# Queries and keys of the second block: where the squares, the gains and the norm's factor are applied

## The reference

```python
q, k, v, p = jnp.split(h @ w_in, [...], axis=-1)
q = rope_2d(rms_norm_2(q.reshape(bsz, seq, N_Q_HEADS, HEAD_DIM), q_gain), row_ang, col_ang)
k = rope_2d(rms_norm_2(k.reshape(bsz, seq, N_KV_HEADS, HEAD_DIM), k_gain), row_ang, col_ang)
...
kc = rms_norm_2(kc.reshape(bsz, n_ctx, N_KV_HEADS, HEAD_DIM), k_gain)     # context keys: no rotation
# rms_norm_2(x, gain) = x * rsqrt(mean(x*x) + EPS) * gain, per head
# rope_1d: x1, x2 = halves; concat(x1*cos - x2*sin, x2*cos + x1*sin)
```

## Time and profile before

| | |
|---|---|
| median of 3 runs | 2244.4 us (2242.2 to 2245.37) |
| the profiled execution | 2244.1 us, its span 2242.5 us |
| PE busy | 2044.5 us (91%) |
| DVE, ACT, POOL busy | 794.9, 580.6, 715.6 us |
| mean granted TensorE clock | 0.951 of full speed |

### The profile page before, as it was taken

How to read it: one execution, slowest core, us unless ns; L and a number is a source line. 1 busy time by engine, 2 the same in 40 slices (tenths; PEclk the granted TensorE clock), 3 DMA queues, 4 the chain that set the end, 5 groups by cost and what they waited for, 6 DMA issues and landing times. The chain is left out here.

```text
span 2242.5 us, 23210 instructions
## 1 busy us (share of the span) xinstructions
PE 2044.5 (91%) x7824; PEld 1099.2 (49%) x7824; DVE 794.9 (35%) x1596; ACT 580.6 (26%) x1205; POOL 715.6 (32%) x1055
## 2 busy tenths in 40 slices
PE   7999999999999999999997697995999699778995
PEld 5555555555564555555542355653444344344442
DVE  1434534432123444433315358533222300442223
ACT  3234331234113442221511114521111211111110
POOL 4766766756766676600000031000110100001101
PEclk9999999999999999999998798996999799878997
DMA  7234343234343244360112600016995621055994
GB/s 301 84 113 150 133 145 119 95 127 145 127 150 111 90 166 144 119 266 38 48 75 104 220 16 22 1 46 279 349 366 210 226 75 38 0 226 227 369 366 165
DMA packets 71119, 339.29 MB, mean 151 GB/s; under 512 B 8760, under 2 KB 10230, under 8 KB 56694
## 3 DMA queue, kind: packets, MB, share of 16 engines
q1 hardware_dynamic: 38502, 217.48, 25.7%
q0 software_dynamic: 27920, 103.82, 13.1%
q10 hardware_dynamic: 4608, 16.78, 1.8%
HBM read 292.97 MB, written 45.09 MB: 151 GB/s over the span
## 5 line engine op out<-in xcount | busy, mean ns | idle before, releaser
L386 PE MATMUL psA<-gB,ring 128*128 128x512 f32 x1024 | 455.1, 597 | 0.0
L324 POOL TENSOR_TENSOR wm<-wm,cs 128x256 f32<-128x256 f32 x448 | 266.3, 627 | 135.4 <-DMA wm<-in_mod_w 134.8
L386 PEld LDWEIGHTS psA<-gB,ring 128*128 128x128 f32 x1024 | 189.5, 190 | 223.8 <-issue 223.8
L328 POOL TENSOR_TENSOR wm<-wm 128x256 f32<-128x256 f32 x336 | 243.8, 753 | 31.1 <-issue 23.1
L378 PE MATMUL psA<-ring,gB 128*128 128x384 f32 (+1 forms) x768 | 242.9, 474 | 1.2 <-ACT gB L665 1.2
L378 PEld LDWEIGHTS psA<-ring,gB 128*128 128x128 f32 x768 | 144.6, 190 | 92.0 <-issue 6.8
L1326 POOL DMA_INDIRECT arena<-xs_scratch,idx x4 | 3.9, 965 | 446.7 <-issue 446.7
L842 DVE COPY probT<-psT 128x512 f32<-128x512 f32 x96 | 65.9, 686 | 159.4 <-PE psT L367 159.4
L1460 PE MATMUL psSO<-wreg,arena 128*128 128x512 f32 x256 | 115.3, 593 | 1.9 <-DVE arena L1986 1.9
L1445 PE MATMUL psA<-wreg,arena 128*128 128x512 f32 x256 | 114.9, 602 | 0.0
L1402 PE MATMUL psA<-wreg,mixT 128*128 128x512 f32 x256 | 113.1, 602 | 1.6 <-issue 0.8
(11 more groups left out here) (283 smaller groups left out, 2790.6 us busy)
## 6 DMA issues: line engine op xcount, KB each, us to landing
wm<-in_mod_w POOLq DMA_DIRECT2D x56, 1024.0 KB, 7.9
wreg<-in_w_gu SPq DMA_DIRECT2D x16, 2048.0 KB, 8.6
wreg<-in_w_dn SPq DMA_DIRECT2D x32, 1024.0 KB, 12.3
ring<-in_w_qk SPq DMA_DIRECT2D x24, 1024.0 KB, 4.9
mixT<-in_w_gu SPq DMA_DIRECT2D x8, 2048.0 KB, 8.6
aT<-in_w_gu SPq DMA_DIRECT2D x8, 2048.0 KB, 8.5
ys_scratch<-arena ACTq DMA_DIRECT2D x32, 512.0 KB, 9.9
ring<-in_w_v SPq DMA_DIRECT2D x8, 1536.0 KB, 6.9
```

Source lines behind the costliest of these rows:

```text
L324: nc.gpsimd.tensor_tensor(wm[:, b, k], wm[:, b, k], c_all[:, k].to_broadcast([P, MCH]), ALU.mult)
L328: nc.gpsimd.tensor_tensor(wm[:, b, k], wm[:, b, k], wm[:, b, n + k], ALU.add)
L386: m = nc.tensor.matmul(psA[:, n % 2, :], w(i), src[:, k, :], start=(i == 0), stop=(i == len(ks) - 1))
```

## The change

Four things are done in another way.

1. ACT squares the values straight from the projection's bank, in front of the copy out of the same bank: eight heads for a query tile, two for a key tile, each into one of the two buffers of `sq` in turn. The squares behind the last copy are gone.
2. DVE multiplies the gains into the rotation's tables, once, before the first reduction: in place for the queries (`rope2`), into a second table in `xm` for the keys (`rope_k`). The sine tables take the gains of the swapped half.
3. DVE reduces and rotates each tile as soon as ACT has copied it, with temporaries in `xm` (`by_cos`, `by_sin`) in place of `sq`. Context keys get the gain only.
4. The factor of the norm is applied last, to tiles that are already rotated; a rotation is linear, and the factor is one number per head and token.

```diff
+    by_cos, by_sin = flat_xm[:, 0:512], flat_xm[:, 640:1152]
+    rope_k = flat_xm[:, 1280:1792].rearrange("p (c t n) -> p c t n", c=2, t=NT)
...
+            def squares(n, src, cols, i):
+                act.wait_ge(a_ready, n + 1)
+                if i >= 2:
+                    act.wait_ge(sq_used, i - 1)
+                nc.scalar.activation(sq[:, i % 2, cols], src, ACT.Square).then_inc(sq_ready, 1)
+
+            for t in range(NT):
+                squares(t, psA[:, t % 2, :], slice(0, 512), t)
                 copy_out(t, qk[:, t, 0:512], psA[:, t % 2, :])
             for n in range(NT + CT):
                 bank = psA[:, n % 2, :]
-                act.wait_ge(a_ready, A_KV + n + 1)
+                squares(A_KV + n, bank[:, 0:P], slice(512, 640), NT + n)
...
-            act.drain()
-            for t in range(NT):
-                if t >= 2:
-                    act.wait_ge(sq_used, t - 1)
-                nc.scalar.activation(sq[:, t % 2, :], qk[:, t, :], ACT.Square).then_inc(sq_ready, 1)
-            act.wait_ge(sq_used, 3)
-            nc.scalar.activation(sq[:, 0, 0:CT * P], kc[:, :, :].rearrange("p t n -> p (t n)"), ACT.Square).then_inc(sq_ready, 1)
-            act.wait_ge(sq_used, 5)
+            act.wait_ge(sq_used, 2 * NT + CT)
             nc.scalar.activation(rmsh[:], ssh[:], ACT.Sqrt, scale=1.0 / HD, bias=eps[:]).then_inc(hd_rms, 1)
...
+            dve.wait_ge(tab_loaded, 16 * 8)
+            dve.wait_ge(t_ready, T_CTX)
+            for i, table in ((1, rope_k), (0, rope2)):
+                for t in range(NT):
+                    nc.vector.tensor_tensor(table[:, 0, t, :], rope2[:, 0, t, :], gains[:, i, :], ALU.mult)
+                    for c in range(2):
+                        nc.vector.tensor_tensor(swapped_halves(table[:, 1, t, :])[:, :, c, :], swapped_halves(rope2[:, 1, t, :])[:, :, c, :],
+                                                swapped_halves(gains[:, i, :])[:, :, 1 - c, :], ALU.mult)
+                dve.drain()
...
+            def roped(x, n, table, t):
+                a, b = by_cos[:, 0:n * HD], by_sin[:, 0:n * HD]
+                nc.vector.tensor_tensor(heads(a, n), heads(x, n), across(table[:, 0, t, :], n), ALU.mult)
...
+            for t in range(NT):
+                sum_squares(t, slice(0, 512), 8, 10 * t)
+                dve.wait_ge(a_copied, t + 1)
+                roped(qk[:, t, 0:512], 8, rope2, t)
+            for t in range(NT):
+                sum_squares(NT + t, slice(512, 640), 2, 10 * t + 8)
+                dve.wait_ge(a_copied, A_KV + t + 1)
+                roped(qk[:, t, 512:640], 2, rope_k, t)
+            for t in range(CT):
+                sum_squares(2 * NT + t, slice(512, 640), 2, 40 + 2 * t)
+            dve.wait_ge(a_copied, A_CTX + CT)
+            nc.vector.tensor_tensor(all_kc, all_kc, across(gains[:, 1, :], 4), ALU.mult)
             dve.wait_ge(hd_rms, 1)
             nc.vector.reciprocal(rsh[:], rmsh[:])
             dve.drain()
+            nc.vector.tensor_tensor(all_kc, all_kc, down(rsh[:, 40:44], 4), ALU.mult)
             for t in range(NT):
                 nc.vector.tensor_tensor(heads(qk[:, t, :], 10), heads(qk[:, t, :], 10), down(rsh[:, 10 * t:10 * t + 10], 10), ALU.mult)
             dve.drain()
...
             dve.sem_inc(qk_ready, 1)
```

More of the change, by code:

```diff
@@ L2033, in heads @@
                 return x.rearrange("p (h n) -> p h n", h=n)
[L2035 to L2044, removed]
             def across(x, n):
@@ L2050, in down, with swapped_halves @@
                 return x.rearrange("p (h o) -> p h o", o=1).to_broadcast([P, n, HD])
+            def swapped_halves(x):
+                return x.rearrange("p (b c n) -> p b c n", b=2, c=2)
+            dve.wait_ge(tab_loaded, 16 * 8)
[7 more added lines that the diff above has]
+                dve.drain()
@@ new lines, in sum_squares @@
+            def sum_squares(i, cols, n, at):
+                dve.wait_ge(sq_ready, i + 1)
+                nc.vector.tensor_reduce(ssh[:, at:at + n], heads(sq[:, i % 2, cols], n), AX.X, ALU.add).then_inc(sq_used, 1)
+            def roped(x, n, table, t):
+                a, b = by_cos[:, 0:n * HD], by_sin[:, 0:n * HD]
+                nc.vector.tensor_tensor(heads(a, n), heads(x, n), across(table[:, 0, t, :], n), ALU.mult)
+                halves = "p (h b c n) -> p h b c n"
+                sizes = dict(h=n, b=2, c=2)
+                for c in range(2):
+                    sin = table[:, 1, t, :].rearrange("p (o b c n) -> p o b c n", o=1, b=2, c=2)[:, :, :, c, :]
+                    nc.vector.tensor_tensor(b.rearrange(halves, **sizes)[:, :, :, c, :], x.rearrange(halves, **sizes)[:, :, :, 1 - c, :],
+                                            sin.to_broadcast([P, n, 2, 16]), ALU.mult)
+                dve.drain()
+                nc.vector.tensor_tensor(x, a, b, ALU.add)
+                dve.drain()
@@ L2052, in _ @@
+            dve.wait_ge(a_copied, A_CTX + CT)
+            all_kc = heads(kc[:, :, :].rearrange("p t n -> p (t n)"), 4)
+            nc.vector.tensor_tensor(all_kc, all_kc, across(gains[:, 1, :], 4), ALU.mult)
+            dve.wait_ge(hd_rms, 1)
+            nc.vector.reciprocal(rsh[:], rmsh[:])
+            dve.drain()
+            nc.vector.tensor_tensor(all_kc, all_kc, down(rsh[:, 40:44], 4), ALU.mult)
             for t in range(NT):
                 nc.vector.tensor_tensor(heads(qk[:, t, :], 10), heads(qk[:, t, :], 10), down(rsh[:, 10 * t:10 * t + 10], 10), ALU.mult)
-            nc.vector.tensor_tensor(all_kc, all_kc, down(rsh[:, 40:44], 4), ALU.mult)
@@ L2055, in _ @@
             dve.drain()
[L2056 to L2073, removed]
```

## The result

The changed kernel takes 2232.64 us (median of 6 runs, 2230.63 to 2235.8), the kernel before, run beside it, 2245.56 (6 runs). The ratio is 0.9943, 95% interval 0.9927 to 0.9959: 0.6% faster, 12.9 us by the medians. 2231.3 had been forecast, in a range of 2228.5 to 2235.5. The profiled execution took 2230.95, its span 2229.4 (mean granted clock 0.955), against 2242.5 before: 13.1 us less.

What follows compares the result with a forecast made beforehand. PE, busy 91%, was taken to bound the kernel with its gaps; 11.8 us for the qk_ready wait plus 1.2 for the clock made 13.0 saved, so 2231.3 us, range 2228.5 to 2235.5.

Steps and rivals of the forecast that it cites:

- The wait for `qk_ready`: PE's wait for DVE before the transposes of keys and queries: it goes whole, 11.8 us saved.
- Squares: ACT's squares ahead of its copies cost the copy's price, 0.60 us for 512 columns, 0.28 for 128; PE not held.
- Tables: DVE's 24 added products on the rotation tables take 5 us, at most 9.8, and cost PE 0.
- A query tile: DVE's reduction and rotation per query tile take 3.3 to 5.5 of 6.9 us, under PE's projections.
- A key tile: DVE's five instructions per key tile take 2.4 of 3.5 us, under PE's projections.
- The clock: PE's transposes up to scores(0) run at the full clock: 1.2 us saved, ends 0 and 1.9.
- The chain of copies: DVE's copies after the first transpose: second key copy at 1.8 us, queries 1 at 4.0, scores(0) at 4.5.
- Early attention runs cold: Rival, chance 0.14: the clock falls in attention's thin start, costing at most 2.9 us; time 2232.5 to 2235.4.
- Two of the signs named in advance: Granted clock 1.00 through transposes and attention; the same length from scores(0) to the end.
- Not passed on: Rival, chance 0.04: a later stage waits for something not shifted, so the gain is lost; 2238 to 2244.
- slower: Rival, chance 0.03: DVE crowded during projections, ACT's squares hold the banks, PE stalls 23.6 us; 2255.
- POOL beside attention: POOL's last four adds run beside attention's start and may hold a DVE division: 0, at most 1 us.

Runs made afterwards that it cites:

- e4: Kernel before, with 13 unread products of 128x512 put into PE's wait for qk_ready; 2246.09 us, ratio 1.0004.
- e5: Changed kernel, with 2 and 3 unread products of 128x512 in PE's two idle stretches around scores(1); 2231.37 us, ratio 0.9935.
- e10: Changed kernel timed again, nothing altered, beside the kernel before on another chip; 2232.66 us, ratio 0.9949.
- e9: Changed kernel, with 38 unread adds of 512 columns on POOL while DVE does its per-tile work; 2235.85 us, ratio 0.9965.
- e2: Kernel before, with one added line: POOL waits for qk_ready before its pooling sums; 2232.26 us, ratio 0.9941.
- e7: Changed kernel, with PE's transposes, scores(0) and scores(1) placed between the pooling products; 2225.44 us, ratio 0.9910.

## Why the prediction was right

**The wait for `qk_ready`, 11.8 us.** Right: 11.96 in the profile. Its parts held. Squares cost 0.60 and 0.28, the copy's price. Tables took 3.0 us (1266.33 to 1269.3), under the 5 taken and far from the bound of 9.8. A query tile took 2.7 us, below the 3.3 to 5.5: the reduction, the product and the add of 512 columns took 0.69 each, where the prediction had 0.79 and 0.82 from rows of 640, and two sine products of 256 took 0.75, where its lower end had 0.82. A key tile took 1.3 of the 2.4. `qk_ready` came at 1319.9, forecast 1319.5, in a run whose pooling products ended 0.9 later.

**The clock, 1.2 us.** Right where it was looked for: 1.45 in the changed kernel, 1.4 alone in e4. The chain of copies that the prediction wrote out is what the DVE rows show, a little faster: both key copies done 1.7 us behind the first transpose (forecast 1.8), queries 1 at 3.6 (4.0), `scores(0)` at 4.25 (4.5).

**Early attention runs cold.** This was a rival with 0.14 and 0 to 2.9 us, taken as an alternative to the forecast. It came about together with it: 1.32 us, shown by e5 to be the clock. The failed step is "against it: it stayed at 0.99 through this very stretch". Before, that stretch came right behind a rise of the clock (0.95 at 1359 to 1360), and in the changed kernel behind transposes with gaps of 0.6. Whether the missing rise or these gaps decide is not shown. Two of the signs named in advance failed with it: a clock of 1.00 through attention, and the same length from `scores(0)` to the end. So the clock's two terms, -1.45 and +1.32, all but cancel, and the sum should have read about 12. That the forecast of 13.0 met the median's 12.9 is partly luck: in the profiles the change itself gives 12.1, and the other 1.0 comes from rows that it does not touch. e10 measured 11.3.

**Not passed on; slower.** Neither came. The slower rival's price, 23.6 us, was wrong by its whole size: e9 made its condition true and PE lost nothing. I had charged each narrow product, and the reduction, with the crowded time of a wider product (a reduction beside POOL kept its 0.69), and left out that ACT may run two tiles ahead.

**POOL beside attention, 0, at most 1 us.** Right: POOL's last instruction started at 1349.67, the first division at 1354.38, and it took 1.15. e2 and e7, where POOL does run beside divisions, show the price: 2.2 to 2.5 us a pair. The lock rule of the Trainium skill (page "SBUF — State Buffer", section "SBUF: two separate sides") agrees with these rows for products with two SBUF inputs. The division has one SBUF input, and by the page it would take the lock only in a two-port mode; it is crowded here too, and no row names its mode. Reductions (0.69 in e9) and copies out of PSUM (0.68 at 1358.11 in e2, beside POOL) went free.

What the prediction did not see is how little of the change the 11.8 us needed. It said that "part of those 38 us is no work of DVE's own", but did not ask how much. e2 shows 15.9 of 37.8 us, more than the wait, and one line of delay for POOL buys the same time as the whole change.

## What to carry to other kernels

When an engine's tail behind the last bank holds the critical engine, compare the same instruction's duration with and without GpSimd running before moving anything: if the difference summed over the tail is the wait, delaying GpSimd's work is a rival to every rewrite. Work moved under a cover wants its margin counted in tiles of room, not in the price of single instructions. And a margin gained (here 22 us) is worth less as margin than as leave to reorder the critical engine, which gave 7 us more here (e7).

## What the runs showed of the hardware

In these traces a granted clock of 1.00 outlasts the same thin stretch or does not, depending on what came before. PE busy 3.15 of 8 us behind a fresh rise (the kernel before): no fall. PE busy 3.13 of 7.5 us behind transposes with gaps (the changed kernel): a fall to 0.50, which lasts 3 to 7 us in the six profiles named above. What a warm arrival gained (1.4 us) the fall took back (1.3), so the gap's removal was worth the gap and nothing for the clock.

Beside GpSimd's adds of 512 columns (e9; alone in the changed kernel), most DVE instructions with two SBUF inputs take 0.5 to 1.1 us more each, and the narrow ones pay about as much as the wide: 1.42 us for a pair of 64 columns (0.35 alone), 1.40 for one of 128 (0.29), 2.89 for a pair of 256 (0.75), 1.60 for one of 512 (0.69), 7.30 for four of 640 (3.02). So the same columns in many small instructions beside GpSimd cost more than in a few wide ones.
